# Bonus rows spread by DMA and multiplied on GpSimd; one accumulator pair finished ahead in the first bodies; softmax steps placed later

## Reference

```python
# first block: attention over 8 heads of 128, trailing-window means, w_o, gated FFN (5632)
# second block, layer 0: RWKV-7 mixer, 32 heads of 64
r, k, v, g = ((x + xx * mu_s) @ w_in[s] for s in range(4))
y = wkv7_scan(r, decay, k, v, kk, a)             # S = S*w - (S kk)(a kk)^T + v k^T ; y = S r
y = (y - mean) * rsqrt(var + GN_EPS) * gn_g + gn_b      # per head
bonus = sum(r * k * r_k, per head) * v           # one number per head and token, times v
x = layernorm(ALPHA * x + ((y + bonus) * silu(g)) @ w_out)
# then k_shared, v_shared and layer 1: differential attention, w_qg, w_out, layer norm
```

## Time and profile before

| what | value |
|---|---|
| median of 3 runs | 2333.85 us (2333.53 to 2334.11) |
| the profiled execution | 2331.94 us, its span 2329.9 us |
| TensorE busy | 2211.3 us, 95% of the span |
| VectorE, ScalarE, GpSimd busy | 1495.9, 1084.2, 66.2 us |
| mean granted TensorE clock | 0.983 of full speed |
| chain that ended last | TensorE 87%, VectorE 8%, ScalarE 3% |
| DMA | 380.74 MB, mean 163 GB/s |

### The profile page before, as it was taken

One profiled execution on the slowest core, in us unless ns is written; L12 is line 12 of the kernel. 1 busy time (PEld: TensorE's weight loads), 2 busy tenths in 40 slices (PEclk: granted clock), 3 DMA queues, 4 the chain that ended last, 5 costly groups with the idle time before them and its releaser, 6 DMA issues.

```text
span 2329.9 us, 39909 instructions
## 1 busy us (share of the span) xinstructions
PE 2211.3 (95%) x15488; PEld 1893.8 (81%) x15488; DVE 1495.9 (64%) x2047; ACT 1084.2 (47%) x1534; POOL 66.2 (3%) x51
## 2 busy tenths in 40 slices
PE   6999989999999999997999999999898999999996
PEld 5888868888888888886887888888777788888885
DVE  5656568885588757866863897924465544566654
ACT  4444555444444434445546565423333534456533
POOL 0700000000000000000000000000100000000000
PEclk9999989999999999998999999999999999999998
DMA  8654445655666556654564656521154455644551
GB/s 265 206 156 152 155 136 172 189 189 187 186 188 189 188 189 190 188 161 148 165 206 130 190 157 190 193 80 22 39 182 140 154 186 187 187 145 145 170 173 63
DMA packets 391141, 380.74 MB, mean 163 GB/s; under 512 B 34081, under 2 KB 389537, under 8 KB 390177
## 3 DMA queue, kind: packets, MB, share of 16 engines
q1 hardware_dynamic: 391010, 378.90, 52.2%
HBM read 372.16 MB, written 6.68 MB: 163 GB/s over the span
## 4 chain that ended last, share of the span: by engine, by line
PE 87%; DVE 8%; ACT 3%; issue 2%; DMA 1%; SPq 0%; DVEq 0%; ACTq 0%
PE acc L690 43%; PE acc L693 21%; PE acc L715 4%; PE acc L977 3%; PE aux L977 3%; PE acc L770 2%; PE acc L771 2%; PE acc L772 2%; PE acc L718 2%; DVE w_lo L1769 2%; ACT w_hi L1182 1%; PE aux L788 1%; PE aux L929 1%; PE aux L1104 1%; PE aux L895 1%
## 5 line engine op out<-in xcount | busy, mean ns | idle before, releaser
L1769 DVE TENSOR_TENSOR w_lo<-raw_w,w_hi 128x1024 fp32r<-128x1024 f32 (+1 forms) x592 | 714.0, 1226 | 485.7 <-ACT w_hi L1182 484.6
L1182 ACT ACTIVATE w_hi<-raw_w 128x1024 fp32r<-128x1024 f32 (+1 forms) x592 | 613.2, 1046 | 714.3 <-PE acc L693 582.6
L690 PE MATMUL acc<-h,w_hi 128*128 128x512 f32 x1664 | 526.3, 398 | 7.1 <-DVE w_lo L1769 4.5
L693 PEld LDWEIGHTS acc<-h,w_lo 128*128 128x128 f32 x1664 | 312.6, 188 | 73.8
L693 PE MATMUL acc<-h,w_lo 128*128 128x256 f32 x1664 | 327.0, 278 | 0.0
L690 PEld LDWEIGHTS acc<-h,w_hi 128*128 128x128 f32 x1664 | 254.5, 189 | 8.9 <-DVE w_lo L1769 5.0
L690 PE MATMUL acc<-x_split,w_hi 128*128 128x512 f32 x704 | 225.3, 401 | 1.7 <-DVE k_shared L1828 1.7
L690 PE MATMUL acc<-ff,w_hi 128*128 128x512 f32 x704 | 222.7, 398 | 2.4 <-DVE ff L2014 2.4
L690 PE MATMUL acc<-xs_b,w_hi 128*128 128x512 f32 x512 | 162.5, 399 | 1.7 <-DVE w_lo L2207 0.9
L693 PEld LDWEIGHTS acc<-ff,w_lo 128*128 128x128 f32 x704 | 133.0, 189 | 31.5
L693 PEld LDWEIGHTS acc<-x_split,w_lo 128*128 128x128 f32 x704 | 132.2, 188 | 31.2
(11 more groups left out here) (332 smaller groups left out, 3174.1 us busy)
## 6 DMA issues: line engine op xcount, KB each, us to landing
raw_w<-in_w_up SPq DMA_DIRECT2D x176, 512.0 KB, 3.5
raw_w<-in_a_w_in SPq DMA_DIRECT2D x128, 512.0 KB, 3.6
raw_w<-in_w_in SPq DMA_DIRECT2D x64, 512.0 KB, 3.9
raw_w<-in_w_down SPq DMA_DIRECT2D x64, 512.0 KB, 3.5
raw_w<-in_b_w_qg SPq DMA_DIRECT2D x64, 512.0 KB, 3.8
raw_w<-in_w_o SPq DMA_DIRECT2D x32, 512.0 KB, 3.6
raw_w<-in_a_w_out SPq DMA_DIRECT2D x32, 512.0 KB, 3.6
raw_w<-in_w_k_shared SPq DMA_DIRECT2D x32, 512.0 KB, 3.5
```

What stands on the lines that cost most here:

```text
L690: pe.matmul(ACC[2 * b + f], WHI[:, q, k, f * P:(f + 1) * P], op[:, kt, :, :].rearrange("p h t -> p (h t)"), start=first, stop=False)
L693: mm = pe.matmul(ACC[2 * b + f][:, 0:T], WLO[:, slot, k, f * P:(f + 1) * P], op[:, kt, 0, :], start=False, stop=last)
L1182: act.activation(WHI[:, u % 4, 0:ku, :], RAWW[:, u, 0:ku, :], ACT.Copy).then_inc(hi_made, 1)
L1769: dve.tensor_tensor(WLO[:, u, 0:ku, :], RAWW[:, u, 0:ku, :], WHI[:, u % 4, 0:ku, :].bitcast(F32), ALU.subtract)\
```

## The change

**Bonus.** `bonus_wide` and VectorE's multiplication are gone from the scan, and with them the wait of `turns` for `bon_done`. SyncE stores `BONR` to DRAM during the products before the scan (n = 84) and in the scan, for g = 0 to 3 at n = 2 to 5, loads the rows spread over the partitions into `BON` (`spread_bonus`, two DMAs of 256 KB, the later ones behind a wait for GpSimd's previous product). GpSimd multiplies four tiles at a time by V, in place (128x1024). The eight units of a_w_out are loaded one at a time at n = 6 to 13 (`first_unit`), no longer ahead of the scan. `operand_lo(0)` moves into the last step, ahead of its `head_pair`.

**First bodies.** At the last depth the order becomes (pr 0, b 0), (pr 1, b 0), (pr 0, b 1), (pr 1, b 1), so b=0 is complete two half units before b=1, and `gates[7]` is waited for one half unit earlier. Both `split`s evacuate b=0 after two split units of the next body, not three.

**Softmax.** The maximum and the exponentials stand at `MAX_AT`, one unit later than before for heads 0 to 5 (the last two unchanged); the normalisation at `NORM_AT`, again one unit later for those.

```diff
+        MAX_AT = [15, 16, 23, 24, 31, 32, 35, 35]
+        NORM_AT = [16, 17, 24, 25, 32, 33, 36, 36]
...
@@ SyncE
+                if n == 84:
+                    sp.wait_ge(rows_out, 1)
+                    sp.dma_start(b_dram, BONR[:, :]).then_inc(bon_stored, 16)
...
-            def first_eight(w):
-                for n in range(8):
-                    sp.wait_ge(unit_done, seen(unit_done))
-                    sp.dma_start(RAWW[:, n, :, :], ...).then_inc(landed[n], 16)
+            def first_unit(n, w):
+                sp.wait_ge(unit_done, seen(unit_done))
+                sp.dma_start(RAWW[:, n, :, :], ...).then_inc(landed[n], 16)
+
+            def spread_bonus(g):
+                if g:
+                    sp.wait_ge(bon_done, 4 * g)
+                rows = b_dram.rearrange("(i r) t -> r i t", r=32)
+                for h_ in range(2):
+                    sp.dma_start(BON[64 * h_:64 * h_ + 64, 4 * g:4 * g + 4, :], rows[2 * g + h_:2 * g + h_ + 1].broadcast_to([64, 4, T]))\
+                      .then_inc(bon_in, 16)
...
-            first_eight(h["a_w_out_2"][0])
+            sp.wait_ge(bon_stored, 16)
             for n in range(2, 4 * NCH):
                 sp.wait_ge(y_done, n - 1)
                 load_t(n)
+                if n < 6:
+                    spread_bonus(n - 2)
+                elif n < 14:
+                    first_unit(n - 6, h["a_w_out_2"][0])
                 if n >= 7 and n % 4 == 3:
                     spread_rows(n // 4 - 1)
@@ GpSimd
+            for g in range(4):
+                pool.wait_ge(bon_in, 32 * (g + 1))
+                b4 = BON[:, 4 * g:4 * g + 4, :]
+                pool.tensor_tensor(b4, b4, V[:, 4 * g:4 * g + 4, :], ALU.mult).then_inc(bon_done, 4)
             pool.wait_ge(g_ready, 8)
@@ TensorE, first_body
-                    for pr in range(2):
-                        pe.wait_ge(*gates[2 * x + pr])
-                        for b in range(2):
+                    halves_of = [(0, 0), (0, 1), (1, 0), (1, 1)] if x < 3 else [(0, 0), (1, 0), (0, 1), (1, 1)]
+                    for pr, b in halves_of:
+                        if b == 0:
+                            pe.wait_ge(*gates[2 * x + pr])
@@ TensorE, turns and step
-                if n > 1:
-                    pe.wait_ge(bon_done, n - 1)
-                elif n:
+                if n:
                     pe.wait_ge(vc_ready, n)
...
-                bonus_wide(n)
@@ ScalarE and VectorE, gemm
-                    split(0, ku, between=lambda: out(0, 0, 7))
+                    split(0, ku, between=lambda: out(0, 0, 7), at=2)
@@ ScalarE, VectorE, beside attention
-                for h_ in heads_at(n, SCORES_AT, 2):
+                for h_ in heads_at(n, MAX_AT):
                     softmax_max(h_)        # ScalarE: exps(h_)
-                for h_ in heads_at(n, SCORES_AT, 3):
+                for h_ in heads_at(n, NORM_AT):
                     softmax_norm(h_)
@@ VectorE, step
-                dve.wait_ge(bon_wide, n + 1)
-                dve.tensor_tensor(BON[:, n, :], AUX[2][:, T:], V[:, n, :], ALU.mult).then_inc(bon_done, 1)
+                if not more:
+                    operand_lo(0)
...
-            operand_lo(0)
             operand_lo(1)
```

More of the change, by code:

```diff
@@ L698, in pairs_of, with first_body @@
                 return [(sem_, base + p_ + 1) for p_ in range(8)]
[L700 removed]
+            def first_body(op, gates, after={}, depth=(0, 1, 2, 3)):
                 for x, q in enumerate(depth):
[L703 to L723 removed]
@@ new lines, in first_body @@
+                    halves_of = [(0, 0), (0, 1), (1, 0), (1, 1)] if x < 3 else [(0, 0), (1, 0), (0, 1), (1, 1)]
+                    for pr, b in halves_of:
+                        if b == 0:
+                            pe.wait_ge(*gates[2 * x + pr])
+                        if pr == 0:
+                            pe.wait_ge(lo_made, seen(lo_made))
+                        if x + pr == 0:
+                            pe.wait_ge(acc_free, seen(acc_free, 2))
+                        for k in (2 * pr, 2 * pr + 1):
+                            kt, first, last = 4 * q + k, x + k == 0, x + k == 6
+                            for f in range(2):
+                                pe.matmul(ACC[2 * b + f], WHI[:, (2 * x + b) % 4, k, f * P:(f + 1) * P],
+                                          op[:, kt, :, :].rearrange("p h t -> p (h t)"), start=first, stop=False)
+                            for f in range(2):
+                                mm = pe.matmul(ACC[2 * b + f][:, 0:T], WLO[:, 2 * x + b, k, f * P:(f + 1) * P], op[:, kt, 0, :],
+                                               start=False, stop=last)
+                        if pr == 1:
+                            mm.then_inc(unit_done, 1)
+                            if 2 * x + b in after:
+                                after[2 * x + b]()
@@ L1182, in split_unit, with split @@
                 act.activation(WHI[:, u % 4, 0:ku, :], RAWW[:, u, 0:ku, :], ACT.Copy).then_inc(hi_made, 1)
-            def split(b, ku=KU, between=None):
+            def split(b, ku=KU, between=None, at=3):
                 for q in range(4):
-                    if q == 3 and between is not None:
+                    if q == at and between is not None:
                         between()
@@ L2252, in read_rest, with operand_lo @@
                 ins.then_inc(rest_out, 1)
+            def operand_lo(g, half=None):
+                dve.wait_ge(gn_hi, g + 1 if half is None else 4 + half)
+                a, b = (4 * g, 4 * g + 4) if half is None else (4 * g + 2 * half, 4 * g + 2 * half + 2)
+                dve.tensor_tensor(C4L[:, a:b, :], BET[:, a:b, :], C4H[:, a:b, :].bitcast(F32), ALU.subtract).then_inc(gn_ready, b - a)
             def step(n):
```

37 lines of the change are left out of this document (5 added, 32 removed).

## The result

The changed kernel takes 2305.41 us (median of 4, 2304.94 to 2306.19) beside 2333.69 for the kernel before (4 runs, same chip): ratio 0.988, interval 0.986 to 0.990, 28.3 us faster. Forecast 2307.4, range 2302.5 to 2314. Its profiled execution is 2305.76 us, the span 2304.1.

A forecast was written before the change was run, and what follows sets the result against it. The prediction took TensorE, busy 95% of the span, as the bound. Its terms, 8.7 + 3.7 + 11.5 + 1.6 + 3.4 - 2.5 = 26.4 us, off 2333.85 gave 2307.4 us, range 2302.5 to 2314.

The forecast's parts named there:

- Bonus matmuls, 15 x 0.58 = 8.7: Scan: TensorE's bonus groups of 0.58 us go with nothing in their place, 8.7 us less over 15 steps.
- Wide rows, -2.5: Scan: head rows' spreading loads land 2.3 us later behind a_w_out units; 1.0 and 1.5 us lost, bounds 0 to 5.
- if the wide rows come later than 2.3 us: Sign in the scan that would prove the prediction wrong: the spread head rows delayed by more than 2.3 us.
- what the DMAs cost: Step on SyncE's list in the scan: moved a_w_out units delay the head rows' store and load, costing 2.5 us.
- End of the scan, 3.7: Scan's end to wkv_out product: with operand_lo(0) first, TensorE starts at 1685.5 instead of 1689.20, 3.7 us gained.
- First bodies, 11.5: Product bodies: waits for the tile just evacuated go, 10.0 us, plus 0.1 for xs_a and 1.4 for w_up.
- clock, 1.6: From b_w_out's second body: the fall to 1.2 GHz behind a 2.6 us wait goes, 1.6 us gained, two chances in three.
- Softmax, 3.4: Softmax one unit later: TensorE's waits for low parts go, 1.5 + 1.5 us, plus 0.4 for heads 4 and 5.
- The first (0.22): Rival, scan steps 1 and 2: GpSimd's product holds up VectorE's state's product, 3.8 us lost, 2311.2 us; chance 0.22.
- The second (wide rows hidden): Rival, scan: the delay of the head rows ends in VectorE's slack, 2304.9 us; chance 0.22.
- The third: Rival, first bodies: evacuation returns as another wait, the 10.0 and 1.6 us don't come, 2319.0 us; chance 0.10.
- The fourth: Rival, scan: transfers bound it, TensorE waits for inverse blocks each step, slower at 2343 us; chance 0.02.

The follow-up runs named there:

- the last kernel of this study: Changed kernel with spread_rows ahead of a_w_out's unit, x's reload later, xs_a's evacuation at its old place, GpSimd waiting for the state's product in steps 1, 2: 2296.10 us.
- the kernels with the first bodies and the softmax alone: Two kernels: the kernel before with only the first-body part, 2317.11 us, and the kernel before with only the softmax part, 2329.16 us.

## Why the prediction was right, and where not

*Bonus matmuls, 15 x 0.58 = 8.7.* Mechanism right, the term too small. The chain's 0.58 is the group's own piece; it also holds apart its neighbours. Before, with the bonus in the middle, and the last kernel of this study, without:

```profile
1552.24 0.63 PE L977 MATMUL acc<-wkv_small,wkv_u 64*64 64x64 f32 x16
1552.80 0.65 PE L929 MATMUL aux<-bonus_rows,consts 32*64 32x256 f32 x4
1553.38 0.68 PE L977 MATMUL aux<-wkv_small 64*64 64x64 f32 x16
1553.90 0.63 PE L977 MATMUL aux<-wkv_s,r_kappa 64*64 64x64 f32 x16
```

```profile
1548.18 0.63 PE L1000 MATMUL acc<-wkv_small,wkv_u 64*64 64x64 f32 x16
1548.65 0.63 PE L1000 MATMUL aux<-wkv_small 64*64 64x64 f32 x16
1549.12 0.63 PE L1000 MATMUL aux<-wkv_s,r_kappa 64*64 64x64 f32 x16
```

From the group before the bonus to the second behind it are 1.66 us, and 0.94 without it: 0.72 each, 10.8 us in 15 steps. Steps 1, 4, 6, 8, 10 and 14, which nothing else touches, are shorter by 0.71 to 0.73.

Step 9 is shorter by 1.97, and there "VectorE loses 16 multiplications, which were off the path" was wrong. It is the step in which ScalarE takes the square root of the head variances and the first unit of a_w_out is split. Before, VectorE's bonus product (1618.87, 1.80 us of waiting for L929 in front of it) stood ahead of the variance and its reciprocal in VectorE's list. ScalarE's root was as late, behind it `WHI` and then the copy of `wkv_x`, for which TensorE paused 1.07 us. Before, then after:

```profile
1621.45 0.42 ACT L1601 ACTIVATE head_rstd_rows<-head_rstd_rows 128x256 f32<-128x256 f32 x1 [2.44 <-DVE head_rstd_rows L2287]
1623.18 0.68 PE L977 MATMUL aux<-wkv_x,inverse_blocks 64*64 64x64 f32 x16 [1.07 <-issue]
```

```profile
1606.96 0.42 ACT L1613 ACTIVATE head_rstd_rows<-head_rstd_rows 128x256 f32<-128x256 f32 x1 [0.47 <-DVE head_rstd_rows L2304]
1608.70 0.67 PE L997 MATMUL aux<-wkv_x,inverse_blocks 64*64 64x64 f32 x16
```

The root starts 2.82 us behind the step's first square before (1618.63), 0.85 after (1606.11). Every trace with VectorE's bonus product in the step has 10.68 there, every trace without it 8.71. That is 1.25 us more than the bonus group itself, and steps 5 and 13, at the same place of their groups, are 0.3 each.

*Wide rows, -2.5.* Right in kind, too small; by the prediction's own sign ("if the wide rows come later than 2.3 us") this term was wrong. The rows came 3.2 us later, not 2.3: 1592.17 is 13.8 behind the square that ends step 5 (1578.36), 1601.41 was 10.6 behind (1590.78). TensorE lost 1.84, not 1.0, and at the second place 1.15 plus the clock that fell behind the wait. Against the kernel before less 0.72 a step these cost 2.1 (step 7) and 3.5 (steps 11 and 12), 5.6 together; against the kernel with GpSimd behind the state's product, whose own step 11 is still 9.22, 4.3. The prediction had 5 at the most; it asked for the clock behind b_w_out's wait and not behind this one.

*What was missed: the reload of x.* The step that failed is "what the DMAs cost": it went through the queue behind each moved load, and did not ask which later wait of SyncE had its cause removed. `bon_done` held 2 MB back until the scan's end. Step 15 is 9.74; after 8.71 with a bonus of 0.72 in it, 8.0 would have been due, so 1.75 were lost against this trace of the kernel before. But that step ran at a granted clock of 0.85; the same step took 7.27 and 7.63 at 1.00 in the kernels with the first bodies and the softmax alone, and beside these, or beside the 6.71 of the kernel with GpSimd behind the state's product, some 3 us were lost.

The 4.8 of the scan, against the kernel before step by step: 10.8 for the bonus groups, 1.9 more in steps 5, 9 and 13, less 5.6 (wide rows), 1.75 (step 15) and 0.6 in steps 2 and 3, which is not explained. The forecast's 6.2 held 8.7 and 2.5 of these. That it came within 1.4 us is luck: what it missed on the gaining side, 4.0, met 5.4 on the other.

*End of the scan, 3.7.* The number is exact, the reason half wrong. (In the traces of the first bodies and the softmax alone the product starts 3.66 behind the last square, not 4.13, so beside them 3.2 were gained.) TensorE starts behind the last square, as said; but it was VectorE's last bonus product and its wait that went, and the moved low part does nothing.

*First bodies, 11.5, and clock, 1.6.* All ends right: waits of 1.3, 1.3, 1.8, 1.7, 2.6, 2.6 gone, xs_a's 1.7 exchanged for 1.6, the clock whole. Alone they gave 14.5, forecast 13.1, with 1.7 and 1.4 of clock in it that this part does not explain. *Softmax, 3.4:* 2.5. Up to the scan 1.1 more came than forecast. Two things of 0.7 stand behind it: h's first bodies wait 15.9 us for `w_lo` instead of 16.6 (the change touches nothing at the start), and mix's first body is held for 1.7 instead of 2.4, as in the kernel with the softmax part alone.

*Rivals.* The first (0.22) did not happen in either trace of the changed kernel, but in 6 of the 9 traces of its family; "escapes by 0.2 us" was read as a likely escape, and hangs on landing times that differ by more than that. Its price, 1.9 us of TensorE a step, was right for full overlap (1.78), and a step usually pays less. The second (wide rows hidden) is refuted: they cost more. The third is refuted but for xs_a. The fourth was not seen: no step waited for inverse blocks.

## What to carry to other kernels

When a producer is moved ahead of time, list the waits that it used to hold shut: each of them now opens early, and what stands behind (here 2 MB) meets whatever is latency-bound at that hour. Small store-and-reload chains go ahead of bulk loads in a queue. An escape by some tenths of a microsecond between two engines whose start hangs on a DMA is no escape: a wait in front of the one with time to spare rules the collision out, and here it cost nothing that the runs could show. An instruction that looks off the path can still stand in front of one that is on it once in sixteen steps: look at each kind of step, not at one. And read what a group of matmuls costs from the spacing of its neighbours, not from its own row.

## What the runs showed of the hardware

VectorE's product of 128x256 with both inputs in SBUF, started inside a GpSimd product, ended 0.27 to 0.29 us behind it in all six cases, whether 0.77 or 2.34 us of the product were left; the subtraction of 128x512 in the kernel before ended 0.54 behind the earlier trace rows. Where VectorE's product had started first, by 0.25 to 0.35 us, both kept their lengths within 0.03 us (three traces). A wide load of two times 256 KB took 7.1 us beside a 2 MB load issued 2.2 us later, 5.5 alone. In the changed kernel, TensorE's wait of 1.15 us in step 11 was followed by 3.4 us at the lower level of the clock (granted clock 0.91 over 20 us); in the second profile of the same kernel one of 1.25 us at the same place was followed by none (1.00). A short wait can take the clock with it, and does so in some executions only.
